# First-stack norms: GpSimd adds up six of eight tiles and their squares instead of four

## The chip, the cores and the metric

One core of a Trainium2 chip runs the whole program in one launch. The metric is the time of the program in microseconds (us). The kernel before takes 1381.66 us, the median of three runs. The engines are named as in the profile: PE is TensorE (matmul), PEld its weight loads, DVE is VectorE, ACT is ScalarE, POOL is GpSimd, SP issues the weight DMAs.

## What is computed

Two stacks of two layers each over 256 tokens of width 1024. The change concerns the first stack alone, and in it the first of the two layer norms of each layer:

```
for l in range(DEPTH):                       # DEPTH = 2
    proj = h @ w_in[l]
    mixed = concat([nsa_mixer(...), gla_mixer(...), pool_mixer(...)])
    h = layer_norm(DEEPNORM_ALPHA * h + mixed @ w_out[l], ln1_g[l], ln1_b[l])     # norm m = 0, 2
    ff = square(relu(h @ w_up[l])) @ w_down[l]
    h = layer_norm(DEEPNORM_ALPHA * h + ff, ln2_g[l], ln2_b[l])                   # norm m = 1, 3

def layer_norm(x, g, b):
    mu = mean(x, -1)
    var = mean(square(x - mu), -1)
    return (x - mu) * rsqrt(var + LN_EPS) * g + b
```

The second stack (`second_block`, two layers with an RG-LRU and attention mixer, a Mamba mixer and gated feed-forwards) is not touched.

## The kernel before

Activations lie transposed: 128 of the 1024 features on the partitions, the 256 tokens along the row, so an activation is KT = 8 tiles of 128x256 and a weight product makes one such tile after another in a PSUM bank. A product in float32 accuracy takes three f16 matmuls for each 128x128 block of weights (lines 744 to 746: high part by high part, high by low, low by high). The weights stream in slots of 128x2048 float32 (`raw`). For each slot ACT writes the f16 high part (`high`, L1768), and DVE the f16 rest (`low`, L2511). The instruction streams of the engines are written out by hand, one function for each engine, and meet at semaphores. Nothing is reordered by a scheduler.

The output product of a layer is `out1_l`, whose eight tiles are made in four pairs. As each tile is done, DVE adds it to the scaled residual in `m_all` (L2584, called the eviction of tile t below, and the one that `evac_value` counts). Layer norms sum over the features, which means over partitions and over the eight tiles. A matmul with a constant matrix `mean` (L969, float32) sums over the partitions and puts the mean on all of them. One such matmul for each tile would do; to save some, POOL first adds up several tiles elementwise: `gather` adds `m_all[:, t]` into `root` (L3387) and the squares in `sq_all[:, t]`, made by ACT (L1817), into `sq_all[:, 0]` (L3392). The last add of squares raises `ln_acc`. All adds of `gather` are in one chain: each waits until the one before it has landed (`tell.settle()`).

PE takes the sums in two places:

- `late()` runs inside the last tile of `out1_l`, after six of its eight weight blocks. It waits for `ln_acc`, sums `root` and `sq_all[:, 0]`, and then each tile between `added_up(m)` and KT - 2 singly, with its squares.
- `finish()` runs after the first twelve matmuls of the next product, `up1_l` (k = 0 of its first four tiles, in `abreast_raw`). It sums tiles 6 and 7 and their squares. The matmul of tile 7 waits for DVE's eviction of that tile, with the squares behind it on PE.

The next product starts on operands that are not yet normalised: ACT (`raw_part`, L1808) and DVE (`raw_low`, L2547) split `m_all * g` into f16 parts, and DVE corrects the four tiles later. The normalised operand (`x_lo`, DVE L2617) is wanted from tile 4 of `up1_l` on.

On DVE the order around the norm is, after the evictions of tiles 4 and 5: `raw_low` for tiles 0 to 3 (one L2544 and four L2547), the low part of a weight slot (L2511), the eviction of tile 6, `raw_low` of tiles 4 and 5, the eviction of tile 7. A float32 matmul of L969 appears as two records in the trace ("x2"), one `mean_of` call each.

Of the kernel before, what the change touches and what calls it, by code (L numbers as in the profile page):

```python
# [29 lines left out]
KT = D // P  # L30
# [345 lines left out]
def two_stacks(nc, stream, small, params, consts, x_t, meta_t, out_t):  # L376
# [14 lines left out]
    with ExitStack() as ctx:  # L391
# [281 lines left out]

        def added_up(m):

            return 6 if m % 2 else 4

        def gathered_of(n):

# [56 lines left out]
        def _(pe):  # L736
# [238 lines left out]
            def layer_norm(name, m):  # L975
# [14 lines left out]
                def late():  # L990
                    pe.wait_ge(ln_acc, m + 1)
                    mean_of(5, root[:, 0:S], S, True, False)
                    mean_of(4, sq_all[:, 0, 0:S], S, True, False)
                    for t in range(added_up(m), KT - 2):
                        sums(t)
# [2353 lines left out]
        def _(pool):  # L3349
# [30 lines left out]
            def gather(name, m):  # L3380

                first, total = products[name]["first"], root[:, 0:S]
                pool.wait_ge(shifted, m + 1)
                tiles = added_up(m)
                for t in range(1, tiles):
                    pool.wait_ge(*evac_value(first + t))
                    tell(pool.tensor_tensor(total, m_all[:, 0, 0:S] if t == 1 else total, m_all[:, t, 0:S], ALU.add))  # L3387
                    tell.settle()
                    if t >= 3:
                        pool.wait_ge(sq_ready, squares_of(m) + (4 if t == 3 else 6))  # L3390
                        for i in ((1, 2, 3) if t == 3 else (t,)):
                            tell(pool.tensor_tensor(sq_all[:, 0, 0:S], sq_all[:, 0, 0:S], sq_all[:, i, 0:S], ALU.add),  # L3392
                                 ln_acc if i == tiles - 1 else None)
                            tell.settle()
# [263 lines left out]
```

## Time and profile before

| | |
|---|---|
| median of 3 runs (lowest, highest) | 1381.66 us (1381.32, 1383.81) |
| the profiled execution: its time | 1381.62 us |
| its span, first to last instruction | 1379.8 us |
| granted TensorE clock, mean | 0.999 of full speed |
| PE busy | 98% of the span |
| DVE busy | 75% |
| ACT busy | 64% |
| POOL busy | 36% |

The times of single instructions below are counted from the start of the span. The profiled execution takes 1.8 us more than its span, before the first instruction and after the last.

### The profile page before, as it was taken

What the parts mean: (1) busy time and instruction counts of PE and PEld (TensorE: products, weight loads), DVE (VectorE), ACT (ScalarE), POOL (GpSimd) and SP (SyncE); (2) the same over time, 40 slices, a digit from 0 to 9 for tenths busy, and PEclk for the clock granted to TensorE, in tenths of its full rate; (3) what the DMA queues carried; (4) which work ended last, traced back from release to release, by engine and by line L of the source; (5) the groups of instructions that cost most, each with busy time, mean ns of one, the idle gap of its engine ahead of it and who ended that gap; (6) DMA issues with size and microseconds to landing.
All of it is one profiled execution on the core that took longest, in us unless ns stands there. A gap on an engine that the chain in (4) does not pass through costs nothing.

```text
span 1379.8 us, 31437 instructions
## 1 busy us (share of the span) xinstructions
PE 1352.9 (98%) x13296; PEld 1160.5 (84%) x13296; DVE 1037.1 (75%) x1465; ACT 879.2 (64%) x1442; POOL 492.8 (36%) x402
## 2 busy tenths in 40 slices
PE   9999999999999999999999999999999999999997
PEld 7778888887778888888778888889888778988887
DVE  6897975569898854568887988756978866898853
ACT  5686764447665863446895755555787888675652
POOL 0143760124146830225210566503114211366610
PEclk9999999999999999999999999999999999999999
DMA  9543566544443656525336365552643334375551
GB/s 366 186 145 132 179 222 211 192 156 156 141 146 139 234 197 214 188 100 172 123 112 225 141 221 189 169 195 93 222 145 123 108 123 148 129 253 207 198 168 32
DMA packets 37020, 234.64 MB, mean 170 GB/s; under 512 B 4752, under 2 KB 7824, under 8 KB 10384
## 3 DMA queue, kind: packets, MB, share of 16 engines
q1 hardware_dynamic: 36880, 232.63, 49.0%
q8 instruction: 105, 1.72, 0.5%
q14 instruction: 35, 0.29, 0.1%
HBM read 231.57 MB, written 1.05 MB: 169 GB/s over the span
## 4 chain that ended last, share of the span: by engine, by line
PE 78%; DVE 12%; ACT 6%; issue 2%; POOL 1%; DMA 1%; SPq 0%; ACTq 0%; DVEq 0%; POOLq 0%
PE psum L744 22%; PE psum L746 22%; PE psum L745 22%; DVE low L2511 4%; PE psum L848 1%; PE psum L850 1%; PE psum L849 1%; PE psum L969 1%; ACT high L1768 1%; ACT m L2219 1%; PE psum L973 1%; POOL h L3414 1%; POOL m L3412 1%; DMA raw<-stream 1%; DVE arena L2666 1%
## 5 line engine op out<-in xcount | busy, mean ns | idle before, releaser
L2511 DVE SCALAR_TENSOR_TENSOR low<-raw,high 128x2048 f16<-128x2048 f32 (+5 forms) x247 | 518.9, 2107 | 180.2 <-ACT high L1768 179.5
L744 PE MATMUL psum<-u,high 128*128 128x256 f16 (+2 forms) x1924 | 529.8, 275 | 0.6 <-ACT arena L1754 0.4
L746 PE MATMUL psum<-u,low 128*128 128x256 f16 (+2 forms) x1924 | 529.5, 275 | 0.0
L745 PE MATMUL psum<-u,high 128*128 128x256 f16 (+2 forms) x1924 | 529.5, 275 | 0.0
L1768 ACT ACTIVATE high<-raw 128x2048 f16<-128x2048 f32 (+4 forms) x248 | 418.2, 1689 | 119.5 <-PE psum L746 89.8
L744 PE MATMUL psum<-arena,high 128*128 128x256 f16 (+3 forms) x1208 | 331.0, 274 | 1.7 <-DVE arena L3111 1.4
L746 PE MATMUL psum<-arena,low 128*128 128x256 f16 (+3 forms) x1208 | 330.9, 274 | 0.0
L745 PE MATMUL psum<-arena,high 128*128 128x256 f16 (+3 forms) x1208 | 330.9, 274 | 0.0
L744 PEld LDWEIGHTS psum<-u,high 128*128 128x128 f16 x1924 | 188.1, 98 | 32.5 <-issue 3.7
L745 PEld LDWEIGHTS psum<-u,high 128*128 128x128 f16 x1924 | 188.3, 98 | 27.9 <-issue 0.7
L746 PEld LDWEIGHTS psum<-u,low 128*128 128x128 f16 x1924 | 188.2, 98 | 27.3
L3014 DVE SCALAR_TENSOR_TENSOR arena<-psum,par,arena 128x271 f32<-128x271 f32 (+3 forms) x296 | 143.3, 491 | 22.5 <-ACT arena L2347 9.8
L744 PEld LDWEIGHTS psum<-arena,high 128*128 128x128 f16 (+1 forms) x1208 | 118.4, 98 | 18.5 <-issue 2.7
L745 PEld LDWEIGHTS psum<-arena,high 128*128 128x128 f16 (+1 forms) x1208 | 118.4, 98 | 16.6
L746 PEld LDWEIGHTS psum<-arena,low 128*128 128x128 f16 (+1 forms) x1208 | 118.4, 98 | 15.3
L2167 ACT ACTIVATE arena<-psum,par 128x272 f32<-128x272 f32 (+1 forms) x88 | 49.2, 569 | 80.4 <-PE psum L746 77.9
L3403 POOL TENSOR_TENSOR arena<-arena 128x272 f16<-128x272 f32 (+1 forms) x44 | 90.6, 2058 | 3.4
L3401 POOL TENSOR_TENSOR arena<-arena 128x272 f32<-128x272 f32 (+1 forms) x44 | 58.5, 1330 | 87.6 <-DVE arena L3030 87.6
L3453 POOL TENSOR_TENSOR arena<-arena 128x256 f16<-128x256 f32 x64 | 67.9, 1074 | 53.9 <-DVE arena L2856 53.9
L3412 POOL TENSOR_TENSOR m<-m,rstd 128x272 f32<-128x272 f32 (+1 forms) x24 | 19.0, 791 | 138.4 <-ACT rstd L2115 138.4
L850 PE MATMUL psum<-arena,low 128*128 128x136 f16 (+2 forms) x304 | 53.3, 221 | 0.0
L848 PE MATMUL psum<-arena,high 128*128 128x136 f16 (+2 forms) x304 | 53.3, 221 | 0.0
(382 smaller groups left out, 1903.0 us busy)
## 6 DMA issues: line engine op xcount, KB each, us to landing
raw<-stream SPq DMA_DIRECT2D x206, 1024.0 KB, 4.8
raw<-stream SPq DMA_DIRECT2D x8, 768.0 KB, 4.3
raw<-stream SPq DMA_DIRECT2D x5, 512.0 KB, 4.4
raw<-stream SPq DMA_DIRECT2D x2, 896.0 KB, 4.5
con<-consts SPq DMA_DIRECT2D x1, 1437.0 KB, 12.3
h<-x_t SPq DMA_DIRECT2D x2, 512.0 KB, 6.0
raw<-stream SPq DMA_DIRECT2D x2, 448.0 KB, 5.5
misc<-small SPq DMA_DIRECT2D x1, 512.0 KB, 13.4
```

Of the source, the lines that this page charges most:

```text
L744: pe.matmul(out, w_hi, x[0], start=start, stop=False)
L745: pe.matmul(out, w_hi, x[1], start=False, stop=False)
L746: return pe.matmul(out, w_lo, x[0], start=False, stop=stop)
L848: pe.matmul(out, high[:, at:at + w], x[0], start=(k == 0), stop=False)
L850: return pe.matmul(out, low[:, at:at + w], x[0], start=False, stop=(k == prod["kt"] - 1))
L1768: tell(act.activation(high[:, at:at + w], raw[:, off:off + w], ACT.Copy, scale=W_SCALE), high_ready, n=2 if half is None else 1)
L2167: tell(act.activation(buf[:, i % GATED, 0:outputs], bank(BANK[g], ahead, ahead + outputs), ACT.Identity, scale=pcol(f"ffn_w{l}", 2 * 2 * F ...
L2511: tell(dve.scalar_tensor_tensor(low[:, at:at + w], raw[:, off:off + w], W_SCALE, high[:, at:at + w], ALU.mult, ALU.subtract), split_ready ...
L3014: ins = dve.scalar_tensor_tensor(dst[:, lo:outputs], bank(BANK[g], at, at + n), weight(taps_in_all - 1 - back), dst[:, lo:outputs], ALU.mu ...
L3401: tell(pool.tensor_tensor(tmp[:, t % 2, 0:n], a[:, t % depth, 0:n], b[:, t % depth, 0:n], ALU.mult))
L3403: tell(pool.tensor_tensor(lo[:, t, 0:n], tmp[:, t % 2, 0:n], hi[:, t, 0:n], ALU.subtract), f_ready)
L3453: tell(pool.tensor_tensor(f1_lo[:, t, :], f_relu[:, t % 4, :], f1_hi[:, t, :], ALU.subtract), f_ready)
```

## The change

`added_up(m)`, the number of tiles that POOL adds up ahead of `late()`, was 6 for the second norm of each layer (m = 1, 3) and 4 for the first (m = 0, 2). Now it is 6 for all four.

```
         def added_up(m):
 
-            return 6 if m % 2 else 4
+            return KT - 2
```

POOL's `gather` and PE's `late` both read it; the loop of `late` over the single tiles is empty now for all norms.

On POOL, in norm m = 0, four adds are new: tile 4 into `root` (the names are output<-inputs), its squares into `sq`, and the same for tile 5. The last three rows were there before: L3366 takes the mean off `m`, and L3369 writes `h`. Norm m = 2 has the same piece.

```order
 L3387 TENSOR_TENSOR root<-root,m 128x256 x2
 L3392 TENSOR_TENSOR sq<-sq 128x256 x3
+L3387 TENSOR_TENSOR root<-root,m 128x256
+L3392 TENSOR_TENSOR sq<-sq 128x256
+L3387 TENSOR_TENSOR root<-root,m 128x256
+L3392 TENSOR_TENSOR sq<-sq 128x256
 L3366 TENSOR_TENSOR m<-m,root 128x256 x8
 L3369 TENSOR_SCALAR h<-m,par 128x256 x8
```

The new adds stand behind the three adds of squares that ended the chain before, and the last of them is now the one that raises `ln_acc`.

On PE, in `late()` of norm m = 0, inside the last tile of `out1_0`, four matmuls with the constant matrix (`con`) are gone: tile 4, its squares, tile 5, its squares.

```order
 L969 MATMUL psum<-root,con 128x256
 L969 MATMUL psum<-sq,con 128x256
-L969 MATMUL psum<-m,con 128x256
-L969 MATMUL psum<-sq,con 128x256
-L969 MATMUL psum<-m,con 128x256
-L969 MATMUL psum<-sq,con 128x256
 L744 MATMUL psum<-arena,high 128x256
 L745 MATMUL psum<-arena,high 128x256
```

The sum of `root`, which waits for `ln_acc`, stands where it stood, right behind the 18th weight matmul of tile 7; the rest of tile 7 now follows two matmuls later instead of six. The streams of DVE, ACT and SP are unchanged.

## Rows read from the trace of the kernel before

**Rows 1.** The page, part 1: busy time, share, instructions of each engine.

```profile
PE 1352.9 (98%) x13296; PEld 1160.5 (84%) x13296; DVE 1037.1 (75%) x1465; ACT 879.2 (64%) x1442; POOL 492.8 (36%) x402
```

**Rows 2.** Busy time by stretch: length, then busy us of each engine, clock, DMA.

```profile
100.00:200.00 100.00, 100.00 (x910) 88.25 (x909) 82.71 (x113) 68.42 (x108) 63.72 (x51) 1.00 0.52 180
```

**Rows 3.** Timeline of PE, norm m = 0: start, length, engine, line, operation.

```profile
127.14 0.60 PE L969 MATMUL psum<-root,con 128*128 128x256 f32 x2
...
129.73 0.27 PE L744 MATMUL psum<-arena,high 128*128 128x256 f16 x1
...
130.39 0.27 PE L744 MATMUL psum<-arena,high 128*128 128x258 f16 x1
...
131.71 1.03 PE L969 MATMUL psum<-m,con 128*128 128x256 f32 x4
...
133.44 0.27 PE L744 MATMUL psum<-arena,high 128*128 128x258 f16 x1
```

**Rows 4.** Timeline of POOL, norm m = 0: the last two adds of `gather`.

```profile
121.83 0.73 POOL L3392 TENSOR_TENSOR sq<-sq 128x256 f32<-128x256 f32 x1
122.63 2.65 POOL L3392 TENSOR_TENSOR sq<-sq 128x256 f32<-128x256 f32 x1
```

**Rows 5.** Timeline of DVE, norm m = 0.

```profile
122.31 2.39 DVE L2511 SCALAR_TENSOR_TENSOR low<-raw,high 128x2048 f16<-128x2048 f32 x1 [3.00 <-ACT high L1768]
...
124.96 0.41 DVE L2584 SCALAR_TENSOR_TENSOR m<-psum,m 128x256 f32<-128x256 f32 x1
...
125.37 0.47 DVE L2547 SCALAR_TENSOR_TENSOR arena<-m,par,arena 128x256 f16<-128x256 f32 x1
...
126.56 0.47 DVE L2547 SCALAR_TENSOR_TENSOR arena<-m,par,arena 128x256 f16<-128x256 f32 x1
...
127.92 2.29 DVE L2511 SCALAR_TENSOR_TENSOR low<-raw,high 128x2048 f16<-128x2048 f32 x1 [0.89 <-ACT high L1768]
...
131.25 0.42 DVE L2584 SCALAR_TENSOR_TENSOR m<-psum,m 128x256 f32<-128x256 f32 x1
```

**Rows 6.** Timeline of ACT, norm m = 0: squares of tiles 4 and 5.

```profile
125.46 0.63 ACT L1817 ACTIVATE sq<-m 128x512 f32<-128x512 f32 x1 [1.47 <-DVE m L2584]
126.00 1.89 ACT L1768 ACTIVATE high<-raw 128x2048 f16<-128x2048 f32 x1
```

**Rows 7.** Timeline of POOL and of DVE, norm m = 1.

```profile
280.87 0.99 POOL L3392 TENSOR_TENSOR sq<-sq 128x256 f32<-128x256 f32 x1 [1.04 <-ACT sq L1817]
281.94 0.79 POOL L3387 TENSOR_TENSOR root<-root,m 128x256 f32<-128x256 f32 x1
282.81 0.80 POOL L3392 TENSOR_TENSOR sq<-sq 128x256 f32<-128x256 f32 x1
...
281.20 0.95 DVE L2547 SCALAR_TENSOR_TENSOR arena<-m,par,arena 128x256 f16<-128x256 f32 x1
282.07 0.95 DVE L2547 SCALAR_TENSOR_TENSOR arena<-m,par,arena 128x256 f16<-128x256 f32 x1
```

**Rows 8.** Timeline of all engines, norm m = 3: eviction of tile 7, its sum.

```profile
596.69 0.42 DVE L2584 SCALAR_TENSOR_TENSOR m<-psum,m 128x256 f32<-128x256 f32 x1 [1.49 <-PE psum L746]
...
597.17 0.30 PEld L969 LDWEIGHTS psum<-m,con 128*128 128x128 f32 x2 [0.48 <-DVE m L2584]
```

**Rows 9.** Timelines: last low part of the normalised operand; PE's first matmul on it.

```profile
143.71 0.48 DVE L2617 SCALAR_TENSOR_TENSOR u<-m,par,u 128x256 f16<-128x256 f32 x1
...
142.69 0.27 PE L744 MATMUL psum<-u,high 128*128 128x256 f16 x1
```

**Rows 10.** Timelines of POOL, PE and DVE, norm m = 2.

```profile
417.90 2.65 POOL L3392 TENSOR_TENSOR sq<-sq 128x256 f32<-128x256 f32 x1
...
422.40 0.60 PE L969 MATMUL psum<-root,con 128*128 128x256 f32 x2
...
423.19 2.29 DVE L2511 SCALAR_TENSOR_TENSOR low<-raw,high 128x2048 f16<-128x2048 f32 x1 [0.89 <-ACT high L1768]
```

**Rows 11.** PE in one stretch: length, busy us, granted clock, DMA.

```profile
700.00:712.00 12.00, 10.52 (x91) 1.00 0.44 165
```

## The prediction

> **What bounds the kernel now.** I read the shares of the engines first, then busy time by stretch, then the timelines around the norms. PE is busy for 98% of the span [rows 1], and in the hundred microseconds that hold norm m = 0 it is busy for all of them [rows 2]. So the end is set there by PE's own stream: a microsecond of matmuls taken out of it is a microsecond won, provided that PE has no wait in its place; a wait put into it is lost in full. The question is thus whether PE's next wait, the one for `ln_acc` in `late()`, still lies behind it. In the timeline of PE `late()` starts at 127.14 with no idle time before it and ends at 129.73 [rows 3]. POOL's chain had ended at 122.63 + 2.65 = 125.28 [rows 4]: 1.86 us of room.
>
> **What is removed.** `late()` is six float32 sums in 129.73 - 127.14 = 2.59 us, so 0.43 us each. Four go: 1.73 us for each norm, 3.45 us for both.
>
> **What is added.** Four adds on POOL, in one chain, and all before `ln_acc`. One alone takes 0.73 us and the next starts 0.08 us after its end (121.83 to 122.63) [rows 4]. The first can start at 125.28 + 0.08 = 125.36; tile 4 was evicted by then and tile 5, evicted at 124.96 + 0.41 = 125.37, isn't wanted before the third add [rows 5]. The second add needs ACT's squares of tiles 4 and 5, done at 125.46 + 0.63 = 126.09, so just in time [rows 6]. With nothing in the way the last add ends no earlier than 125.36 + 4 x 0.73 + 3 x 0.08 = 128.5. That is 1.4 us after PE arrives, so the room of 1.86 us doesn't cover it, and most of the gain turns into the wait.
>
> **POOL and DVE hold each other up.** POOL's third add of squares took 2.65 us, not 0.73: it was issued inside DVE's 128x2048 pass (122.31 to 124.70) and ended 0.58 us after it [rows 4, 5]. Norm m = 1 shows the same adds beside `raw_low`, which in the new order is what DVE does at this moment. There POOL's adds take 0.99, 0.79 and 0.80 us, and each L2547 takes 0.95 us instead of 0.47 [rows 7]. They take turns, one DVE instruction behind each add, with POOL slowed by 0.06 to 0.26 us and DVE by 0.47.
>
> In m = 0 four L2547 start at 125.37 [rows 5], together with POOL's four adds. Laid out in turns:
> - root + tile 4: 125.36 to 126.09. First L2547 to 126.4.
> - squares 4: the chain and ACT's squares are both ready by 126.2; 126.2 to 127.05. Second L2547 to 127.35.
> - root + tile 5: 127.13 to 127.92. Third L2547 to 128.2.
> - squares 5: 128.00 to 128.8. Fourth L2547 to 129.1.
> `ln_acc` comes at 128.8. If the first L2547 gets in ahead of the first add, all of it ends at 128.95; I take 128.8. PE starts again 0.16 us behind a releaser: in m = 3 the eviction ended at 597.11 and the weight load began 0.06 us later, at 597.17 [rows 8]; I allow 0.1 us more until its matmul runs. So `late()` runs from 128.95 and its two sums end at 129.8, where the six ended at 129.73. **First term: +0.1 us for each norm**, the whole 1.73 us eaten by a wait of 1.8 us.
>
> **What is late next.** DVE. Before, its 128x2048 pass started at 127.92, when ACT's high part was there; now it must wait for the fourth L2547 and starts at 129.0, 1.1 us later. If the first L2547 went first, the pass is held up by the last add instead, and is 0.9 us late. Between the end of this pass (130.21) and the end of tile 7's eviction (131.67) there are only DVE's own instructions, 1.46 us of them [rows 5]. So tile 7 is evicted at 131.3 + 1.46 = 132.75 (132.6 in the other case). Tile 7 itself is finished by then (130.5). `finish()` reaches the sum of tile 7 at 131.71 + 0.43 = 132.14 before the change, 0.5 us behind the eviction [rows 3, 5]; now that sum can't start before 132.75 + 0.16 = 132.9, or 132.75 in the other case. The two sums of squares behind it follow at once, since ACT's squares need 0.42 us from 132.8. The four sums end at 132.9 + 3 x 0.43 = 134.2 instead of 133.44. **Second term: +0.8 us, with 0.6 as its lower case.** The first term doesn't add to it: it moves PE's arrival at 132.14 by 0.1 us, which this wait takes in.
>
> Then the norm's chain. Its start on DVE moves by the 1.1 us of the eviction, PE by 0.8. The operand's last low part ends at 143.71 + 0.48 = 144.19, PE begins the first tile that reads it at 142.69 and comes to the last of its eight blocks 21 matmuls of 0.11 us later, at 145.0 [rows 9]. Of 0.8 us room 0.3 go: no further wait. Nor do the later weight slots matter, which PE wants 5 us apart.
>
> Norm m = 2 repeats the distances of m = 0 to 0.03 us: from the long add's start to `late()` 4.50 us (before 4.51), from `late()` to the pass 0.79 (0.78) [rows 3, 4, 5, 10]. So both layers count alike.
>
> **The sum.** 0.6 to 0.8 us, taken as 0.75, twice: +1.5 us. Against the profiled execution, 1381.62 us (span 1379.8 and 1.8 around it), this is 1383.1; the median of the runs shown, 1381.66, stands 0.04 us above that execution, so the forecast is 1383.1. About 0.2% (2.8 us) is what a measurement of this kernel can tell from no change, so this is no measurable change.
>
> PE's waits, 1.8 and 0.8 us, cost no clock by what the trace shows: with 1.5 us of idle time in twelve the granted clock was 1.00, the 2.4 GHz level [rows 11].
>
> **The rivals.**
> - *The last add falls behind DVE's 128x2048 pass: slower.* In my layout two instructions of DVE would have to slip ahead for this. For it: without mutual delay the last add starts at 125.36 + 3 x 0.81 = 127.8 to 127.9, and the pass at 127.92; a few hundredths decide, and two L2547 in one of POOL's gaps would do it. Against it: in m = 1 every L2547 that met an add was itself held until its end, which pushes the pass out [rows 7]. Point from which it decides: the pass starts before the last add. Price: pass to 130.21, add to 130.79 (0.58 behind it, as for the third), PE from 130.95, its two sums to 131.8: 2.1 us late, and tile 7's eviction then hides behind that. Twice: +4.2 us, 1385.8; in one layer only, 1384.5. The Trainium skill, "SBUF — State Buffer", on the two sides of SBUF, states that DVE with two SBUF inputs and GpSimd take one pair of ports as an exclusive lock for a whole instruction, and that the order of issue decides who blocks. By that rule the 2.65 us row is what one expects (the trace agrees), and this rival is what the rule makes of an add issued behind the pass.
> - *DVE isn't held up: no loss at all.* The adds run at 0.73 us and the L2547 too. Then PE is back at 128.5 + 0.16 and ends its sums at 129.55, 0.2 us early, and tile 7's eviction stays at 131.67: -0.2 to 0 us each, 1381.2 to 1381.7. Rows 7 speak against it.
> - *The removed matmuls are won in full: faster.* -3.45 us, 1378.2. It needs `ln_acc` by 127.14, four adds in 1.8 us, which at 0.73 us each cannot be. It stays possible only if the recorded lengths on POOL are much longer than what the next in the chain waits for; the 0.81 us from start to start speaks against that.
> - *The norm's chain becomes late.* If it moves by more than 0.8 us against PE, a further wait opens before tile 4 of `up1`; I count 0.3. Some 0.5 us more each, 1384.1.
>
> **How the numbers follow.** Forecast 70%; DVE not held up 7%; chain late 6%, partly over the bound; full gain 3%; last add behind the pass in both layers 11%, in one 3%. Faster by over 0.2% needs 1378.9: 3%. Slower by over 0.2% is above 1384.4: 11 + 3 and 2 of the late chain, 16%. The rest, 81%, is within. The likeliest case's own range is 1382.2 to 1384.1 (0.6 to 0.8 us each, and half a microsecond around for runs). The range runs down to 1380.8, under the case in which nothing is held up, and up to 1385.8, the rival on the slow side; it leaves out the full gain and half of that rival.
>
> **What the changed profile would show.** Right: POOL's four new adds at 125.4 to 128.8 with 0.73 to 1.0 us each; the four L2547 at about 0.95; an idle time of PE of 1.8 us before the sum of `root`, released by POOL; L2511 starting near 129.0; tile 7's eviction ending near 132.7 and PE idle some 0.5 to 0.8 us in `finish()` for it; everything later shifted by 0.75 us after the first layer and 1.5 after the second. Wrong: an add of 2.6 us at the end of `gather` (the slow rival); L2547 at 0.47 (no mutual delay); no idle time at 127.14 (the gain is real); an idle time at 143 to 145 (the chain).

## The result and the profile after

The changed kernel takes 1384.32 us in the median of 22 runs (1383.49 to 1385.83), the kernel before 1382.21 us in 22 runs beside them (1381.32 to 1384.18). The ratio is 1.0013, with a 95% interval of 1.0007 to 1.0019: slower by 2.1 us. That is less than the bound of 0.2% that the prediction set for "no measurable change", but the interval leaves 1 out: with 22 runs of each kernel the loss can be told from nothing. The span of the profiled execution is 1381.8 us, 2.0 us more than before.

The timelines of norm m = 0 answer to [rows 3 to 6]. In this execution everything up to the norm runs 0.20 us earlier than in that of before (PE's first L969 begins at 114.06, not at 114.26), so 0.20 is to be added to a time of after before it is set beside one of before. First POOL in the changed kernel: the add that was the last, and the four new ones.

```profile
122.44 2.66 POOL L3392 TENSOR_TENSOR sq<-sq 128x256 f32<-128x256 f32 x1
125.18 0.73 POOL L3387 TENSOR_TENSOR root<-root,m 128x256 f32<-128x256 f32 x1
126.04 0.73 POOL L3392 TENSOR_TENSOR sq<-sq 128x256 f32<-128x256 f32 x1
126.85 0.79 POOL L3387 TENSOR_TENSOR root<-root,m 128x256 f32<-128x256 f32 x1
127.72 0.79 POOL L3392 TENSOR_TENSOR sq<-sq 128x256 f32<-128x256 f32 x1
```

Then DVE of the same kernel, from the first `raw_low` to the eviction of tile 7.

```profile
125.18 1.01 DVE L2547 SCALAR_TENSOR_TENSOR arena<-m,par,arena 128x256 f16<-128x256 f32 x1
126.11 0.95 DVE L2547 SCALAR_TENSOR_TENSOR arena<-m,par,arena 128x256 f16<-128x256 f32 x1
126.98 0.94 DVE L2547 SCALAR_TENSOR_TENSOR arena<-m,par,arena 128x256 f16<-128x256 f32 x1
127.85 0.94 DVE L2547 SCALAR_TENSOR_TENSOR arena<-m,par,arena 128x256 f16<-128x256 f32 x1
128.71 2.28 DVE L2511 SCALAR_TENSOR_TENSOR low<-raw,high 128x2048 f16<-128x2048 f32 x1
...
132.04 0.41 DVE L2584 SCALAR_TENSOR_TENSOR m<-psum,m 128x256 f32<-128x256 f32 x1
```

The engines take turns. Each L2547 is issued while an add of POOL runs and ends 0.28 us after that add's end (125.91 and 126.19, 126.77 and 127.06, 127.64 and 127.92, 128.51 and 128.79). An add loses at most 0.06 us, each L2547 0.47 us or more against its 0.47 alone. The 128x2048 pass had idle time before it in [rows 5]; now it follows the fourth L2547 at once and starts 0.99 us later (128.71 + 0.20 against 127.92). Tile 7's eviction is later by the same 0.99.

PE of the changed kernel: `late()`, what follows it, `finish()`, and the place near 159 that the prediction had passed over.

```profile
128.56 0.70 PE L969 MATMUL psum<-root,con 128*128 128x256 f32 x2 [1.46 <-POOL sq L3392]
129.10 0.59 PE L969 MATMUL psum<-sq,con 128*128 128x256 f32 x2
129.53 0.27 PE L744 MATMUL psum<-arena,high 128*128 128x256 f16 x1
...
131.50 0.60 PE L969 MATMUL psum<-m,con 128*128 128x256 f32 x2
132.50 0.70 PE L969 MATMUL psum<-m,con 128*128 128x256 f32 x2 [0.40 <-DVE m L2584]
133.04 1.03 PE L969 MATMUL psum<-sq,con 128*128 128x256 f32 x4
133.90 0.27 PE L744 MATMUL psum<-arena,high 128*128 128x258 f16 x1
...
159.23 0.28 PE L744 MATMUL psum<-u,high 128*128 128x256 f16 x1 [0.19 <-DVE low L2511]
```

Three readings. After `late()` PE goes on with tile 7 at 129.53 + 0.20 = 129.73, where it was before to the hundredth [rows 3]: the wait has eaten the four matmuls exactly. At the end of `finish()` it stands at 133.90 + 0.20 = 134.10 against 133.44: 0.66 us late, by the wait for tile 7. And at 159.23 it waits for a low part of weights. The bracket says 0.19, but a matmul is on record for 0.27 us while the next begins 0.11 us after it; counted by starts (158.76, and then 159.23 in place of 158.87) 0.36 us are lost. The place in the kernel before, on DVE and PE, shows that there was no room there:

```profile
156.07 2.29 DVE L2511 SCALAR_TENSOR_TENSOR low<-raw,high 128x2048 f16<-128x2048 f32 x1 [1.49 <-ACT high L1768]
...
158.30 0.27 PE L746 MATMUL psum<-u,low 128*128 128x256 f16 x1
158.42 0.28 PE L744 MATMUL psum<-u,high 128*128 128x256 f16 x1
```

The pass ended at 158.36 and PE took its weights at 158.42, at a distance of 0.12 instead of 0.11 from the matmul ahead, with no idle time on record. In the changed kernel, where PE does wait, it starts at the same 0.06 us behind the pass (156.88 + 2.29 = 159.17, and 159.23). So these 0.06 us are no room but what the handover takes: PE and DVE came there together before, and the 1.01 us by which the pass is late now (159.17 + 0.20 against 158.36) is the whole 1.01 us by which PE is late (159.23 + 0.20 against 158.42).

**One measure for all runs.** Two stretches of PE's stream hold the two norms, each between two L969 that are in every kernel: from the shift sum of norm m = 0 to `finish()` of norm m = 1, and from the shift sum of norm m = 2 to `late()` of norm m = 3. The four starts, in the kernel before and in the changed one:

```profile
114.26 0.60 PE L969 MATMUL psum<-m,con 128*128 128x256 f32 x2
302.53 1.03 PE L969 MATMUL psum<-m,con 128*128 128x256 f32 x4
409.52 0.60 PE L969 MATMUL psum<-m,con 128*128 128x256 f32 x2
593.00 0.60 PE L969 MATMUL psum<-root,con 128*128 128x256 f32 x2
```

```profile
114.06 0.60 PE L969 MATMUL psum<-m,con 128*128 128x256 f32 x2
303.34 1.03 PE L969 MATMUL psum<-m,con 128*128 128x256 f32 x4
410.36 0.60 PE L969 MATMUL psum<-m,con 128*128 128x256 f32 x2
594.84 0.60 PE L969 MATMUL psum<-root,con 128*128 128x256 f32 x2
```

Before, the stretches are 188.27 and 183.48 us long; now 189.28 and 184.48: +1.01 and +1.00 us, and the middle is the same to 0.03. Each number is read from one profiled execution. The first layer of e1, which that run leaves as it was, is 0.03 us off, and the two layers agree to 0.03 us in every run that treats them alike, far finer than whole times can show. The same four starts were read in every run ("between" is the stretch from the second start to the third, 106.99 us before):

| run | layer 0, us | between, us | layer 1, us | whole, ratio (interval) |
|---|---|---|---|---|
| the change | +1.01 | +0.03 | +1.00 | 1.0013 (1.0007 to 1.0019) |
| e1 second layer only | +0.03 | +0.11 | +0.98 | 1.0009 (1.0000 to 1.0018) |
| e2 sums left out, no adds | +0.01 | +1.69 | -0.01 | 0.9999 (0.9991 to 1.0008) |
| e3 adds alone | +0.98 | 0.00 | +0.99 | 1.0014 (1.0005 to 1.0023) |
| e4 five tiles | +0.03 | 0.00 | +0.03 | 1.0003 (0.9994 to 1.0011) |
| e5 six, tile 7 first | +0.22 | +1.69 | +0.20 | 1.0003 (0.9994 to 1.0012) |
| e7 before, both moves | -0.02 | +2.04 | -0.04 | 1.0002 (0.9993 to 1.0011) |
| e8 five, both moves | -0.89 | +2.06 | -0.90 | 0.9989 (0.9980 to 0.9998) |
| e9 six, sums in finish() | +0.61 | +0.36 | +0.58 | 1.0011 (1.0002 to 1.0021) |
| e10 six, chain first | +0.63 | -0.01 | +0.62 | 1.0010 (1.0001 to 1.0019) |
| e11 five, moves in m = 0, 2 | -0.89 | +0.01 | -0.90 | 0.9987 (0.9978 to 0.9995) |

In the column "between", the 1.69 us in e2, e5, e7 and e8 are told in the last section, and the 0.35 more in e7, e8 and e9 with e7. The 0.11 of e1 is unexplained.

### The profile page after: what moved, and what is told of

The parts are those of the page before. It is cut to its first block, busy times and chain, and to the rows that moved or that the text cites. A ratio compares the mean times of both kernels' runs of the same rounds, so it can differ in the third digit from the quotient of the medians.

```text
span 1381.8 us, 31421 instructions
## 1 busy us (share of the span) xinstructions
PE 1351.3 (98%) x13280; PEld 1157.7 (84%) x13280; DVE 1041.3 (75%) x1465; ACT 879.9 (64%) x1442; POOL 499.6 (36%) x410
## 4 chain that ended last, share of the span: by engine, by line
PE 71%; DVE 16%; ACT 7%; issue 3%; POOL 1%; DMA 0%; ACTq 0%; DVEq 0%; SPq 0%; POOLq 0%
PE psum L744 20%; PE psum L746 20%; PE psum L745 20%; DVE low L2511 5%; ACT high L1768 2%; PE psum L848 1%; PE psum L849 1%; PE psum L850 1%; ACT m L2219 1%; PE psum L973 1%; DVE arena L2547 1%; DVE u L2617 1%; PE psum L1022 1%; POOL h L3414 1%; POOL m L3412 1%
## 5 line engine op out<-in xcount | busy, mean ns | idle before, releaser
L2511 DVE SCALAR_TENSOR_TENSOR low<-raw,high 128x2048 f16<-128x2048 f32 (+5 forms) x247 | 519.1, 2108 | 177.9 <-ACT high L1768 177.3
```

What stands on the lines that cost most here:

```text
L2511: tell(dve.scalar_tensor_tensor(low[:, at:at + w], raw[:, off:off + w], W_SCALE, high[:, at:at + w], ALU.mult, ALU.subtract), split_ready ...
```

## The experiments

**e1, the second layer alone.**

```
-            return 6 if m % 2 else 4
+            return KT - 2 if m else 4
```

> The change in the second layer alone (six tiles in norm m = 2, four in m = 0). My theory: the loss arises anew at each of the two norms and is the same in both, 1.05 us each: the times of the first layer are those of before, those behind norm m = 2 are later by 1.0 to 1.1 us, and the whole is 1.0 us slower than before. Rival, that one layer's loss hides part of the other's: anything from 0 to 2 us.

Measured: +0.03 us in the first layer, +0.98 in the second, 1383.11 us against 1381.74. The loss arises at each norm for itself.

**e2, the gain alone.** `late()` sums only `root` and `sq`, which hold four tiles. Tiles 4 and 5 are missing in mean and variance.

```
-                    for t in range(added_up(m), KT - 2):
-                        sums(t)
```

> The kernel before, with the four single sums of tiles 4 and 5 left out of late() in norms m = 0 and 2 and nothing added on POOL (the mean and the variance there lack these two tiles). What the removed matmuls are worth by themselves. My theory: nearly nothing. PE comes 1.73 us earlier to finish(), waits there for DVE's eviction of tile 7, which has not moved (sum of tile 7 at 131.8 instead of 132.14), and what is left of the gain, 0.3 us, is lost again at the weight slot that DVE finishes just in time at 158.4: 0 to -0.1 us for each layer, 0 to -0.3 us in all. Rival, that the matmuls are on the path that sets the end and only the wait for POOL ate them: -1.73 us for each layer, -3.5 us in all.

Measured: +0.01 and -0.01 us, 1381.96 us against 1381.74. Four matmuls of 0.43 us fewer on an engine that is busy throughout the stretch, and nothing is won. PE of this run shows where they went:

```profile
126.88 0.60 PE L969 MATMUL psum<-root,con 128*128 128x256 f32 x2
127.31 0.59 PE L969 MATMUL psum<-sq,con 128*128 128x256 f32 x2
130.35 0.70 PE L969 MATMUL psum<-m,con 128*128 128x256 f32 x2 [0.47 <-DVE m L2582]
131.47 0.70 PE L969 MATMUL psum<-m,con 128*128 128x256 f32 x2 [0.42 <-DVE m L2582]
...
158.18 0.28 PE L744 MATMUL psum<-u,high 128*128 128x256 f16 x1 [0.17 <-DVE low L2509]
```

(The edit moves the lines by two: L2582 is the eviction L2584, L2509 the pass L2511.) PE now waits for the evictions of both tile 6 and tile 7, and gives back what it still has in hand after them at the weight slot. So the wait for `ln_acc` didn't take the gain from the path: there was none to take. This is the run that decides between my theory and the rival that PE alone sets the end.

**e3, the cost alone.** PE as before, POOL with four more adds into a spare tile, behind the raise of `ln_acc`.

```
+                for t in range(tiles, KT - 2):
+                    pool.wait_ge(*evac_value(first + t))
+                    tell(pool.tensor_tensor(power[:, 0:S], m_all[:, t - 1, 0:S], m_all[:, t, 0:S], ALU.add))
+                    tell.settle()
+                    pool.wait_ge(sq_ready, squares_of(m) + 6)
+                    tell(pool.tensor_tensor(power[:, 0:S], sq_all[:, t - 1, 0:S], sq_all[:, t, 0:S], ALU.add))
+                    tell.settle()
```

> The kernel before, with six single sums in PE as before, and four more adds on POOL at the place of the new ones, of the same size and with the same waits, but into a spare tile and behind the add that raises ln_acc. PE neither waits for them nor loses a matmul. My theory: the whole loss of the change is here, since DVE is held up by the adds: pass L2511 0.8 us later, eviction of tile 7 1.0 us later, PE idle in finish(), +0.65 us there and +0.4 us more at the weight slot near 158.4; +1.05 us for each layer, +2.1 us in all. Rival, that the loss comes from PE's wait for ln_acc: no change, 0 us.

Measured: +0.98 and +0.99 us, 1384.15 us against 1381.74. The whole loss of the change, without a wait for `ln_acc` and without a matmul less. DVE of this run, where four L2547 take 3.62 us (1.66 alone) and the pass has no idle time before it:

```profile
125.92 3.62 DVE L2547 SCALAR_TENSOR_TENSOR arena<-m,par,arena 128x256 f16<-128x256 f32 x4
129.46 2.28 DVE L2511 SCALAR_TENSOR_TENSOR low<-raw,high 128x2048 f16<-128x2048 f32 x1
```

**e4, five tiles.**

```
-            return 6 if m % 2 else 4
+            return 6 if m % 2 else 5
```

> Five tiles added up by POOL in norms m = 0 and 2, tile 5 summed singly. Two new adds, which end at about 126.9, before PE comes to late() at 127.14, so no wait there, and two matmuls less (0.87 us). Two of the four L2547 are held up by 0.47 us each, and the pass L2511 behind them had 0.9 us of idle time before it, so it starts 0 to 0.1 us later. My theory: the 0.87 us do not arrive, since PE waits for tile 7's eviction and for the weight slot at 158.4: 0 to +0.1 us for each layer, 0 to +0.2 us in all. Rival, that PE's matmuls set the end once no wait for POOL stands there: -0.87 us for each layer, -1.7 us in all.

Measured: +0.03 and +0.03 us, 1382.38 us against 1381.74. The wait for POOL is gone and two matmuls with it; PE gives the 0.87 us back at tile 7 (0.31 us idle on record there) and at the slot (0.17 on record). As expected of the theory, and against the rival.

**e5, six tiles, tile 7 evicted first.**

```
-                        if t == 6 and m % 2 == 0:
+                        if t == 7 and m % 2 == 0:
                             raw_low(m, which, l, range(4, 6))
```

> The changed kernel (six tiles), with one move on DVE: raw_low of tiles 4 and 5 (two L2547, 0.8 us) goes behind the eviction of tile 7 instead of ahead of it. My theory: the 1.05 us lost at each norm come from the eviction of tile 7, and through it from the norm's chain up to the weight slot near 158.4, being late on DVE. The move brings tile 7's eviction back to within 0.2 us of where it was before, PE's wait in finish() goes from 0.4 us to about 0, and the chain behind is that of before: PE is where it was before the change, 0 to +0.2 us for each layer, 0 to +0.4 us against the kernel before in all (2 us less than the changed kernel). Its matmuls are fewer by 1.73 us and its wait for ln_acc is still 1.5 us. Rival, that the loss comes with the wait for ln_acc: +2 us stay.

Measured: +0.22 and +0.20 us instead of +1.01 and +1.00. PE no longer waits in `finish()`: its two sums of tiles are one row without idle time, at 131.56, where before they stood at 131.71 with a start 0.15 us later.

```profile
128.62 0.70 PE L969 MATMUL psum<-root,con 128*128 128x256 f32 x2 [1.46 <-POOL sq L3392]
129.15 0.59 PE L969 MATMUL psum<-sq,con 128*128 128x256 f32 x2
131.56 1.03 PE L969 MATMUL psum<-m,con 128*128 128x256 f32 x4
...
158.15 0.27 PE L746 MATMUL psum<-u,low 128*128 128x256 f16 x1
158.49 0.28 PE L744 MATMUL psum<-u,high 128*128 128x256 f16 x1
```

The wait for `ln_acc` is unchanged at 1.46 us, and four fifths of the loss are gone. The last two rows show the rest: at the weight slot the next matmul begins 0.34 us behind the one before it instead of 0.11. The whole time, 1382.97 us against 1382.06, is within its interval of both 0 and 1 us.

**e10, six tiles, mean and variance first.** It takes the other half of the loss.

```
-                if not last:
+                if m == 1:
                     raw_low(m, which, l, range(6, KT))
...
                 tell(dve.tensor_scalar(rstd[:, 0:S], rstd[:, 0:S], 0.0, None, ALU.max), ln_var)
+                if m % 2 == 0:
+                    raw_low(m, which, l, range(6, KT))
```

> The changed kernel (six tiles), with one move on DVE in norms m = 0 and 2 alone: raw_low of tiles 6 and 7 goes behind the mean and variance (L2601 to L2608). Tile 7 is evicted as late as in the changed kernel. This takes the second half of the loss by itself. My theory: PE's wait for tile 7 in finish() stays, and with it 0.65 us for each layer; the norm's chain is no longer late against PE, so the wait of about 0.2 us and the 0.4 us lost at the weight slot near 159.2 go. +0.65 us for each layer, +1.3 us in all against the kernel before, where the changed kernel has +2.1. Rival, that the slot is late for another reason (ACT, the DMA): it stays at +2.1 us.

Measured: +0.63 and +0.62 us, 1383.25 us against 1382.05. The idle time in `finish()` is still there (0.41 us on record), and there is none between 157 and 160. So the two parts of the loss are 0.63 us for tile 7, which this move leaves in place, and 0.38 us for the norm's chain, which it takes away. The move of e5 takes away the first part and 0.16 us of the second, since an earlier tile 7 also starts the chain earlier.

**e7, both moves in the kernel before.** The first is that of e5. The second is that of e10, but with `if not last` as its condition, so that it is made in norm m = 1 too.

> The kernel before (four tiles), with the move of raw_low of tiles 4 and 5 behind tile 7's eviction, and a second one: raw_low of tiles 6 and 7 goes behind the mean and variance on DVE (L2601 to L2608) instead of ahead of them, in norms 0 to 2. Tile 7 is evicted 0.7 us earlier and the normalised operand and the weight slot near 158.4 are done some 0.8 us earlier. My theory: no gain, since nothing is taken from PE, which had no idle time there: 0 to -0.1 us in all. Rival, that the chain on DVE by itself set the end already: -0.8 us for each layer, -1.6 us in all.

Measured: -0.02 and -0.04 us, 1382.48 us against 1382.06. The moves alone are worth nothing, since PE has its full stream to run. Behind norm m = 1, though, something is lost, as the next run's numbers show too: the middle stretch (302.53 to 409.52 in the kernel before, 106.99 us) is 109.03 us here. Of the excess 1.69 us are another thing, told at the end; 0.35 are the move's. DVE of this run in norm m = 1:

```profile
306.11 1.81 DVE L2547 SCALAR_TENSOR_TENSOR arena<-m,par,arena 128x256 f16<-128x256 f32 x2
```

Two L2547 take 1.81 us where they took 0.88 ahead of the mean, because POOL's subtraction of the mean has begun by then. They take 1.81 us in norm m = 0 of this run too, but there the move brings DVE to the copy of the mean (L2599 here) 0.77 us earlier than before, and in norm m = 1 only 0.11 us earlier. The normalisation is then 0.65 us late behind norm m = 1, and PE waits at a weight slot (0.48 us on record at 318.48).

**e8, five tiles and both moves.**

> Five tiles, with both moves of the run above. The two matmuls less (0.87 us) and the chain on DVE 0.8 us or more earlier come together here, neither of which gains alone. My theory: tile 7's eviction and the weight slot no longer hold PE up, and the removed matmuls arrive: -0.8 to -0.9 us for each layer, -1.7 us in all against the kernel before. Rival, that another engine (ACT, whose order is not changed) holds the chain where it was: 0 us.

Measured: -0.89 and -0.90 us, 1380.73 us against 1382.06. Two things that are worth nothing each, e4 and e7, are worth 0.9 us for each layer together: the two matmuls of 0.43 us arrive in full.

**e11, the same in norms m = 0 and 2 alone** (the conditions of e10 and of e5, five tiles).

> Five tiles with both moves (tiles 4 and 5 behind tile 7's eviction, tiles 6 and 7 behind mean and variance), but in norms m = 0 and 2 alone; norm m = 1 is that of before. The run with both moves everywhere won 0.89 us at m = 0 and 0.90 us at m = 2 in its trace, and lost 0.37 us between 290 and 325, behind norm m = 1. My theory: POOL's subtraction of the mean and raw_low meet there on the shared ports, and without the move in m = 1 the 0.37 us come back: -1.8 us in all against the kernel before. Rival, that the 0.37 us have nothing to do with the move: -1.4 us.

Measured: -0.89 and -0.90 us, and the middle stretch is 107.00 us again. 1380.00 us against 1382.05, ratio 0.9987 (0.9978 to 0.9995): faster than the kernel before by more than its interval, and the lowest median of this study. The step from e8 to e11 shows in the stretch between the norms; the whole times of the two can't be told apart.

**e9, six tiles, the sums of `root` and `sq` in `finish()`.**

```
+                    if m % 2 == 0:
+                        late(True)
                     for t in (KT - 2, KT - 1):
...
+                    if name.startswith("out1") and n == 3:
+                        low_part(i - 1 + SPLIT)
...
+                if not last:
+                    raw_low(m, which, l, range(6 if m % 2 else 4, KT))
```

The lines left out take `late()` from its old place for norms m = 0 and 2, put off the low part of the weight slot, and remove the earlier calls of `raw_low`. The last condition moves `raw_low` of tiles 6 and 7 in norm m = 1 too, as in e7, and the stretch between the norms is 0.36 us longer for it.

> Six tiles; the sums of root and of its squares go from late() to the start of finish(), 18 matmuls later, so that PE has no wait for ln_acc. On DVE both evictions of tiles 6 and 7 come ahead of the 128x2048 pass, and raw_low of tiles 4 to 7 goes behind the mean and variance. My theory: no wait for POOL (the last add at 128.8, the sum at 129.1), four matmuls less, so PE is 1.73 us earlier at the end of finish(); the chain on DVE is earlier by 1.0 to 1.1 us only, as DVE has the same work to do before it, and holds PE at the weight slot near 158.4: -1.0 to -1.2 us for each layer, -2.1 us in all against the kernel before. If the chain moves as far as PE: -3.4 us; if PE still waits for tile 7 or the slot as in the changed kernel: 0.

A miss: +0.61 and +0.58 us instead of -1.0 to -1.2, 1383.72 us against 1382.06. The first part of the theory held. PE has no wait and ends `finish()` 1.73 us earlier than before. Then it waits three times for the norm's chain. DVE and PE of this run:

```profile
133.79 0.75 DVE L2610 TENSOR_SCALAR rstd<-rstd 128x256 f32<-128x256 f32 x1
134.46 3.55 DVE L2553 SCALAR_TENSOR_TENSOR arena<-m,par,arena 128x256 f16<-128x256 f32 x4
137.94 0.86 DVE L2631 SCALAR_TENSOR_TENSOR m<-m,par,psum 128x256 f32<-128x256 f32 x2
```

```profile
143.85 0.28 PE L744 MATMUL psum<-u,high 128*128 128x256 f16 x1 [0.40 <-DVE u L2621]
144.75 0.28 PE L744 MATMUL psum<-u,high 128*128 128x256 f16 x1 [0.40 <-DVE u L2621]
...
159.48 0.28 PE L744 MATMUL psum<-u,high 128*128 128x256 f16 x1 [0.57 <-DVE low L2515]
```

I had put four `raw_low` (L2553 here), which take 1.66 us alone, where DVE had a gap, and forgot that POOL subtracts the mean at just this time (from 132.97 to 139.28 in this run). They took 3.55 us, in turns with POOL, and the normalisation behind them was late. It is the mechanism of the changed kernel over again, at another place.

## Why the prediction was right, and where it was not

*The removed matmuls and the wait.* Forecast: `late()` ends 0.1 us late, after a wait of 1.8 us. Measured: 0.00 us. The last add ended at 128.51 + 0.20 = 128.71 (forecast 128.8) and PE went on 0.05 us after it, not 0.16. The wait on record is 1.46 us; by starts, from 127.14 to 128.76, it is 1.62, and the sum that waited takes 0.54 us up to the next start (128.56 to 129.10) where 0.43 is usual: 1.73 together.

*The turns of POOL and DVE.* Forecast from norm m = 1: adds of 0.73 to 1.0 us, L2547 of 0.95. Measured: 0.73 to 0.79, and 0.94 to 1.01. The rival with the last add behind the 128x2048 pass did not come about in any of the profiled executions, for the reason given: the L2547 that met an add was itself held, and pushed the pass out. The Trainium skill, "SBUF — State Buffer", section "Who interferes with whom", states that a DVE instruction with two SBUF inputs contends with a GpSimd instruction that reads SBUF, and that the one that issues second fully blocks. The trace agrees (every L2547 issued inside an add ends 0.28 us behind it), and e9's 3.55 us too.

*Tile 7's eviction.* Forecast: 1.1 us late, PE 0.8 us late at the end of `finish()`, 0.6 as the lower case. Measured: 0.99 and 0.66; e10 isolates it as 0.63. My range of 0.6 to 0.8 held, my 0.75 was a little high.

*The norm's chain and the weight slots.* This is the step that failed: "Nor do the later weight slots matter, which PE wants 5 us apart", and with it the 0.3 us of the chain's 0.8 us of room. The room at the normalised operand was as computed, but it is not the only place where the chain meets PE. It goes on over the correction of four tiles on DVE and their relu on ACT to the high part and the low part of a weight slot, which was ready just when PE wanted it: there was no room at all. I looked at how far apart PE wants slots, not at when DVE delivers them. It cost 0.36 us in the changed kernel's trace, 0.38 by e10. With it the sum is 1.0 for each layer, not 0.75, and 2.0 in all, not 1.5. The change stayed under the bound of 2.8 us, though 22 runs can tell 2.1 us from nothing, which the prediction thought they couldn't. The time lay within the range, 1.2 us above the predicted 1383.1. Of that 0.76 is this step, less 0.24 by which the term of tile 7 was too high (0.75 against 0.63, twice), and 0.55 is the median of before, which is 1382.21 over 22 runs where three gave 1381.66; the last 0.1 us is open.

One of the rivals had named this mechanism: "The norm's chain becomes late", with 0.5 us more for each layer, 1384.1 and a chance of 6%. It is nearest to what came. But it looked for the wait before tile 4 of `up1_l`, at 143 to 145, where PE has no idle time in the changed kernel; the wait came some 14 us later, at the weight slot. The time was right although the likeliest case lacked a term, since that term was small.

*"a microsecond of matmuls taken out of it is a microsecond won".* This premise was wrong too, and the wait for POOL hid it. It stood under the condition that PE has no wait in its place, but for that wait the prediction looked at `ln_acc` alone, and took the gain of 1.73 us as real and then eaten. e2 shows that without any wait for POOL it is 0.0. PE being busy throughout does not mean that PE alone sets the end: DVE's eviction of tile 7 was 0.5 us ahead of PE, and the weight slot not at all. The rival "The removed matmuls are won in full" was given one condition, `ln_acc` by 127.14; e2 has the sums on time and wins nothing. The forecast's bookkeeping, a gain of 1.73 us against a wait of 1.8, was right for the time only because the two nearly cancel, which was luck: the loss is all DVE's delay, as e3 shows, which has neither.

## What to carry to other kernels

An engine that is busy all the time can still have no slack behind others: before counting removed work as won, look at each place further on where it meets an engine that it doesn't drive, and take the smallest room, here none. Leave the work out in one run, and add only the new work in another; the two together tell more than the change itself. Work handed to POOL is not free for DVE where both read SBUF and DVE does so with two operands: count it twice, once for its chain and once, 0.47 us for each 0.73 us add here, for what DVE does at the same time.

## What the runs showed of the hardware

In the profiled executions of e2, e5, e7 and e8 the middle stretch is 1.69 us longer than in the others (2.04 and 2.06 in e7 and e8, with the 0.35 told at e7). All executions have an idle time of PE of 1.7 us there, for ACT. Behind it the granted clock fell in these four and stayed up in the rest. Busy time and granted clock of PE by stretch, the kernel before and then e2:

```profile
324.00:328.00 4.00, 2.28 (x21) 1.00 0.22 92
328.00:332.00 4.00, 4.00 (x39) 1.00 0.40 104
```

```profile
324.00:328.00 4.00, 2.29 (x21) 1.00 0.16 66
328.00:332.00 4.00, 4.00 (x24) 0.57 0.46 131
332.00:336.00 4.00, 4.00 (x33) 1.00 0.71 233
```

A mean of 0.57 is near the 1.2 GHz level for most of four microseconds, with 24 matmuls where 39 fit at 2.4 GHz. The same idle time is thus followed by 1.69 us of loss in one execution and by none in the next. The single times of the kernel before lie in two groups about so far apart (mostly 1381.3 to 1382.4, and 1383.2 to 1384.2). The mean granted clock on record for them agrees: of the 87 executions beside the experiments, the 24 above 1382.8 us have 0.997 (18) or 0.998 (6), and the 63 below have 0.998 or 0.999. Where in these executions the clock fell is not shown, since they have no trace. The 1.5 us waits of the changed kernel at its two norms did not bring the clock down in its profiled execution.
